# A hybrid decoder block on one core: the attention bias tables built on VectorE inside the first head pair, and small setup work issued earlier on ScalarE

## The chip, the core and the metric

The kernel runs on one NeuronCore of a Trainium2 chip: TensorE (PE), VectorE (DVE), ScalarE (ACT), GpSimd (POOL) and SyncE (SP, which here only issues transfers), 16 DMA engines, SBUF and the eight banks of PSUM. Each engine works through its own instructions in order, and they meet through semaphores. The metric is the device time of one execution in microseconds (us), the median of several runs.

## What is computed

One decoder layer over 256 tokens of width 1024: dilated window attention in three groups and retention side by side, merged through gates and an output projection, then a mixture of 32 experts in 4 groups, and a last RMSNorm. Cut to what matters:

```python
ATTN_GROUPS = ((128, 1), (512, 4), (2048, 16))      # (window, dilation)
h = rms_norm(x, g_mix)
proj = h @ w_in
qa, ka, va, qr, kr, vr, gr_swish, gate_a, gate_r = jnp.split(proj, split_at, axis=-1)
for gi, (window, dilation) in enumerate(ATTN_GROUPS):
    ...
    s = einsum(q, k) * (Dh ** -0.5)
    valid = (rel >= 0) & (rel <= n_back) & ...
    bias = -slopes * (rel * dilation)               # ALiBi, one slope for each of 8 heads
    s = jnp.where(valid, s + bias, -jnp.inf)
    ...
yr = retention_chunkwise(qr, kr, vr)                # decay gamma_h = 1 - 2^(-5-h)
merged = sigmoid(gate_a) * (o_attn @ w_attn_branch) + sigmoid(gate_r) * (o_ret @ w_ret_branch)
x = x + merged @ w_out
h2 = rms_norm(x, g_ffn)
x = x + hier_moe(h2, ...)                           # top-1 group, top-2 experts in it
return rms_norm(x, g_final)
```

With 256 tokens the bias of a group depends only on the distance query minus key: a query may see a key at distance d when 0 <= d <= window and d is a multiple of the dilation. The kernel therefore keeps one table `bias_t` (128 partitions x 3 groups x 256 positions) of minus the distance, or a very large negative number where the key may not be seen, and multiplies it by the slope of the head.

## The kernel before

**Precision.** Projections are made with float32 split in two: ACT rounds a chunk of weights to its high part (`high`, L589 to L596) and DVE subtracts it to get the low part (`low`, L762 to L770). PE then makes three products (high x high, high x low, low x high; `mm3`, L1159). The normed input is split the same way: ACT writes `hT` part 0 (`normed_high(m)`, L604) and DVE part 1 (`normed_low(m)`, L803), for m = 0 to 3, two of the eight 128-row tiles each.

**Units of work.** A "quad" Q is one block of weight columns in four chunks s = 0 to 3, each two of the eight row tiles. SP loads chunk s of quad Q+1 into the raw buffer s as soon as DVE has made the low part of chunk s of quad Q (L385). ACT may overwrite chunk s of the split buffer once PE has used it (`chunk_used`, L594). PE needs for chunk s of a quad the low part of the weights (`lo_ready`, L1183), and for quad 0 also the low part of `hT` (`hT_dve`, L1228). So each chunk goes SP, ACT, DVE, PE.

**The start.** x is loaded; ACT squares and sums it, POOL takes the power -1/2, DVE spreads the result over a diagonal, PE turns it into a row, ACT copies the row to `roots`. PE transposes x. DVE makes the normed tiles (`norm_columns(m)`, L796) from the transposed x and the roots; its order is norm columns 0 and 1, `normed_low(0)`, `low(0, 1)`, `normed_low(1)`, norm columns 2, `low(0, 2)`, `normed_low(2)`, norm columns 3, `low(0, 3)`, `normed_low(3)`. ACT goes `normed_high(m)`, then `high(0, m+1)`. PE fills its idle time with 26 products that nobody reads (`unread`, L1165), the last 18 of them between the roots and the first chunk of quad 0.

**The bias table.** POOL writes the distance as an integer and as a float table (L542, L543). DVE makes the residues of groups 1 and 2 and adds them times the mask value (L782 to L786), all before its first step of the normalisation. POOL cuts the tables to the window with `affine_select` (L566 to L577) after the powers -1/2 of the normalisation. DVE waits for `bias_done` (L819) ahead of the attention loop.

**Attention.** Four head pairs i = 0 to 3, each a query quad 3i, a key quad 3i+1 and a value quad 3i+2. DVE copies the keys `kT` out of PSUM between the second and third `low` of the value quad (L825 to L827), and PE's scores wait for that copy (`ak_ev`, L1237). Then come bias and maximum (DVE), exponent (ACT), scaling (DVE), transposes and the product with the values (PE). On DVE and ACT pairs 0 to 2 are a loop on the engine and pair 3 is written out.

**After it.** Retention in two rounds (`decay` tables from four exponents on ACT, L649 to L652), gates, attention branch, retention branch, output projection, router (whose weights `wr` DVE multiplies by the gain `gain_k`, L926 to L929), and then eight or more passes over teams of four experts, each of which loads 24 MB of weights. SP also loads quarters of the first experts' weights in between (`quarter`, L409).

## Time and profile before

| | us |
|---|---|
| time, median of 3 runs | 776.35 (775.78 to 776.81) |
| the profiled execution | 775.78, of which its span 774.0 |
| PE busy | 581.4 (75%) |
| DVE busy | 241.1 (31%) |
| ACT busy | 183.4 (24%) |
| POOL busy | 10.8 (1%) |
| DMA mean over the span | 329 GB/s |

The span runs from the first to the last instruction of the core; 1.78 us of the profiled execution lie around it. Up to about 333 us PE works nearly without a gap and the DMA engines are busy some two thirds of the time; after that the passes over the experts follow with the DMA engines full at about 425 GB/s and PE waiting in each pass. A row of the timeline shows start, duration, engine, line, operation, written<-read tiles, shape and count, and in brackets how long the engine had been idle and who released it. Instructions of an engine overlap by about 0.1 us in it.

### The profile page before, as it was taken

What the parts mean: (1) busy time and instruction counts of PE and PEld (TensorE: products, weight loads), DVE (VectorE), ACT (ScalarE), POOL (GpSimd) and SP (SyncE); (2) the same over time, 40 slices, a digit from 0 to 9 for tenths busy, and PEclk for the clock granted to TensorE, in tenths of its full rate; (3) what the DMA queues carried; (4) which work ended last, traced back from release to release, by engine and by line L of the source; (5) the groups of instructions that cost most, each with busy time, mean ns of one, the idle gap of its engine ahead of it and who ended that gap; (6) DMA issues with size and microseconds to landing.
All of it is one profiled execution on the core that took longest, in us unless ns stands there. A gap on an engine that the chain in (4) does not pass through costs nothing.

```text
span 774.0 us, 10791 instructions
## 1 busy us (share of the span) xinstructions
PE 581.4 (75%) x4329; PEld 403.8 (52%) x4329; DVE 241.1 (31%) x407; ACT 183.4 (24%) x250; POOL 10.8 (1%) x31
## 2 busy tenths in 40 slices
PE   8999999999999999992960970970870870790795
PEld 8999999989899999840420320320320320320331
DVE  7668486746554457551010010010010010000001
ACT  5455453644425434420000000000000000000002
POOL 3000000000000000000000000000000000000000
PEclk9999999999999999997985895895895895795799
DMA  8966949555537667989999999999999999999995
GB/s 240 274 173 184 273 139 318 163 169 164 168 113 225 221 207 263 364 345 420 431 425 424 431 430 421 432 425 425 428 429 425 428 427 428 426 429 429 424 415 210
DMA packets 86538, 254.84 MB, mean 329 GB/s; under 512 B 8432, under 2 KB 57584, under 8 KB 74608
## 3 DMA queue, kind: packets, MB, share of 16 engines
q1 hardware_dynamic: 84000, 254.30, 85.4%
q10 hardware_dynamic: 2512, 0.18, 0.2%
q8 instruction: 18, 0.29, 0.2%
q14 instruction: 8, 0.07, 0.0%
HBM read 253.41 MB, written 1.05 MB: 329 GB/s over the span
## 4 chain that ended last, share of the span: by engine, by line
PE 64%; DMA 30%; DVE 2%; ACT 2%; issue 1%; SPq 1%; POOL 0%; POOLq 0%; DVEq 0%; ACTq 0%
PE ps L1157 63%; DMA ring<-in_w_down 29%; DVE low_part L766 1%; ACT work L632 1%; ACT high_part L596 1%; DMA ring<-in_w_out 0%; DMA store<-in_x 0%; SPq L508 0%; PE ps L1253 0%; DVE work L960 0%; DVE mid L954 0%; PE ps L1281 0%; PE ps L1363 0%; POOL rstd L539 0%; DVE hn L1135 0%
## 5 line engine op out<-in xcount | busy, mean ns | idle before, releaser
L1157 PE MATMUL ps<-store,work 128*32 128x512 f32 x128 | 71.7, 720 | 176.3 <-DMA ring<-in_w_down 175.6
L1157 PE MATMUL ps<-ring,work 128*32 128x512 f32 x896 | 184.5, 611 | 0.0
L1157 PEld LDWEIGHTS ps<-store,work 128*32 128x32 f32 x128 | 15.6, 130 | 224.7 <-DMA ring<-in_w_down 165.0
L1157 PE MATMUL ps<-hT,split 128*128 128x256 f32 x768 | 93.6, 284 | 0.0
L1157 PEld LDWEIGHTS ps<-hT,split 128*128 128x128 f32 x768 | 92.6, 192 | 0.8 <-issue 0.7
L769 DVE TENSOR_TENSOR split<-ring,split 128x768 fp32r<-128x768 f32 (+1 forms) x72 | 73.9, 1044 | 53.8 <-ACT split L596 53.7
L1073 DVE TENSOR_TENSOR work<-ps,gain_s 128x512 f32<-128x512 f32 x16 | 11.1, 692 | 247.9 <-PE ps L1157 247.9
L596 ACT ACTIVATE split<-ring 128x768 fp32r<-128x768 f32 (+1 forms) x72 | 65.0, 915 | 70.2 <-PE ps L1157 50.4
L1157 PE MATMUL ps<-split,hT 128*128 128x384 f32 (+1 forms) x384 | 80.4, 365 | 0.0
L1157 PEld LDWEIGHTS ps<-split,hT 128*128 128x128 f32 x384 | 68.8, 188 | 7.8
L1157 PE MATMUL ps<-hT_slot,work 128*32 128x512 f32 x128 | 71.7, 720 | 0.0
L1157 PE MATMUL ps<-oRT_slot,work 128*32 128x512 f32 x128 | 71.7, 720 | 0.0
L728 ACT ACTIVATE work<-ps 128x512 f32<-128x512 f32 x16 | 9.6, 597 | 240.7 <-PE ps L1157 240.7
L1157 PEld LDWEIGHTS ps<-ring,work 128*32 128x32 f32 x896 | 46.3, 113 | 38.8 <-issue 38.8
L1157 PE MATMUL ps<-mid,work 128*32 128x512 f32 (+1 forms) x152 | 61.9, 560 | 0.0
L766 DVE TENSOR_TENSOR low_part<-ring,high_part 128x1024 fp32r<-128x1024 f32 x36 | 44.1, 1225 | 46.8 <-ACT high_part L596 46.7
L1157 PE MATMUL ps<-spare,work 128*32 128x512 f32 x128 | 56.4, 594 | 0.0
L596 ACT ACTIVATE high_part<-ring 128x1024 fp32r<-128x1024 f32 x36 | 38.1, 1058 | 53.6 <-DMA ring<-in_w_in 21.9
L1157 PE MATMUL ps<-hT,high_part 128*128 128x256 f32 x256 | 46.3, 284 | 0.0
L1080 DVE TENSOR_TENSOR work<-work,ps 128x512 f32<-128x512 f32 x8 | 5.5, 689 | 130.1 <-PE ps L1157 130.1
L1157 PEld LDWEIGHTS ps<-hT,high_part 128*128 128x128 f32 x256 | 40.0, 192 | 0.1
L1157 PEld LDWEIGHTS ps<-mid,work 128*32 128x32 f32 (+1 forms) x152 | 18.1, 122 | 40.1 <-issue 38.7
(197 smaller groups left out, 691.2 us busy)
## 6 DMA issues: line engine op xcount, KB each, us to landing
ring<-in_w_up SPq DMA_DIRECT2D x23, 2048.0 KB, 38.2
ring<-in_w_gate SPq DMA_DIRECT2D x18, 2048.0 KB, 24.9
ring<-in_w_in SPq DMA_DIRECT2D x80, 256.0 KB, 3.2
ring<-in_w_in SPq DMA_DIRECT2D x96, 192.0 KB, 4.2
mid<-in_w_up SPq DMA_DIRECT2D x8, 2048.0 KB, 34.1
store<-in_w_down SPq DMA_DIRECT2D x7, 2048.0 KB, 17.6
hT_slot<-in_w_down SPq DMA_DIRECT2D x6, 2048.0 KB, 21.8
oRT_slot<-in_w_down SPq DMA_DIRECT2D x6, 2048.0 KB, 26.2
```

Source lines behind the costliest of these rows:

```text
L596: act.activation(high_of, raw(s, n), ACT.Copy).then_inc(hi_ready, 1)
L632: act.activation(probsT[u], s_cols(u), ACT.Copy).then_inc(apt_act, 1)
L728: act.activation(yS[:, h * HALF:(h + 1) * HALF], bank(2 + h), ACT.Copy).then_inc(yS_ev[h], 1)
L766: dve.tensor_tensor(low_part[:, s, 0:n], raw(s, n), high_part[:, s, 0:n].bitcast(F32), ALU.subtract).then_inc(lo_ready, 1)
L769: dve.tensor_tensor(split[:, s, 1, 0:n], raw(s, n), split[:, s, 0, 0:n].bitcast(F32), ALU.subtract).then_inc(lo_ready, 1)
L1073: dve.tensor_tensor(xg[:, steps, :], bank(h).rearrange("p (k s) -> p k s", k=4), gain_s[:, steps].unsqueeze(2).to_broadcast([P, 4, P]), AL ...
L1080: dve.tensor_tensor(hid, sg, bank(3), ALU.mult).then_inc(hid_ready, 1)
L1157: return pe.matmul(o, lhsT=l, rhs=r, start=start, stop=stop, skip_group_check=shared)
```

## The change

It takes the bias table off POOL and makes it on DVE alone, in the head pair that first needs it, and moves some small work.

- POOL loses the float distance table and the four `affine_select`. DVE loses the six steps at its start and the wait for `bias_done`. A new function `bias_of(g)` makes the table of one group in a chain of 8 (group 0) or 5 (groups 1 and 2) instructions on 128x256, each waiting for the one before: convert, mask the residue, compare, add. Its calls stand on DVE in pair 0: group 0 after the second `low` of the key quad, group 1 after the fourth, group 2 between the first and second `low` of the value quad. Pair 0 is written out for this, and the loop runs over pairs 1 and 2.
- On ACT the order in quad 0 is now `normed_high(0)`, `normed_high(1)`, `high(0, 1)`, `normed_high(2)`, `high(0, 2)`, `normed_high(3)`, `high(0, 3)`. DVE's order there stays.
- Four small loads (router weights, router bias and the ffn gain in two layouts) and the four exponents of the decay tables move on ACT from the retention stage to right behind `high(0, 3)`, ahead of `high(1, 0)`.
- DVE multiplies the router weights by the gain right after attention rather than in the gates, and waits for the decay tables there.

The diff, without the line that names the three semaphores that fall away:

```diff
             pool.iota(dist_i[:, :], pattern=[[1, T]], base=-P, channel_multiplier=-1).then_inc(const_ready, 1)
-            pool.iota(dist, pattern=[[1, T]], base=-P, channel_multiplier=-1,
-                      allow_small_or_imprecise_dtypes=True).then_inc(dist_done, 1)
...
             inv_root(0)
-
-            for g, (window, _dil) in enumerate(GROUPS):
...
-                ins = pool.affine_select(out=bias_t[:, g, :], in_=dist if g == 0 else bias_t[:, g, :], compare_op=ALU.is_ge,
-                                         fill=MASKED, base=P, pattern=[[-1, T]], channel_multiplier=1)
-                if window < T:
-                    link(ins)
-                    ins = pool.affine_select(out=bias_t[:, g, :], in_=bias_t[:, g, :], compare_op=ALU.is_ge, fill=MASKED,
-                                             base=window - P, pattern=[[1, T]], channel_multiplier=-1)
-                ins.then_inc(bias_done, 1)
...
             act.activation(roots, bank(4, T), ACT.Copy).then_inc(roots_ev, 1)
-            for m in range(CH):
-                normed_high(m)
-                if m < CH - 1:
-                    high(0, m + 1, W_A)
+            normed_high(0)
+            normed_high(1)
+            high(0, 1, W_A)
+            normed_high(2)
+            high(0, 2, W_A)
+            normed_high(3)
+            high(0, 3, W_A)
+
+            act.dma_start(wr[:, :, :], w_router.rearrange("(k p) n -> p k n", p=P)).then_inc(s_wr, 16)
+            act.dma_start(br[:, :], b_router.partition_broadcast(P)).then_inc(s_wr, 16)
+            act.dma_start(gain_k[:, :], g_ffn.rearrange("(k p) -> p k", p=P),
+                          allow_slow_non_contiguous=True).then_inc(s_gk, 16)
+            act.dma_start(gain_s[:, :], g_ffn.rearrange("(p k) -> p k", k=KT)).then_inc(s_gk, 16)
+            act.wait_ge(age_done, 1)
+            for h in range(RET_HEADS):
+                act.activation(decay[:, h, :], age[:, :], ACT.Exp,
+                               scale=float(np.log1p(-2.0 ** (-5.0 - h)))).then_inc(decay_done, 1)
...
             dve.memset(all_ones, 1.0).then_inc(ones_done, 1)
-            dve.wait_ge(const_ready, 3)
-            dve.wait_ge(dist_done, 1)
-            for g in range(1, NG):
-                link(dve.tensor_single_scalar(resid_i, dist_i, GROUPS[g][1] - 1, ALU.bitwise_and))
-                link(dve.tensor_copy(resid_f, resid_i))
-                dve.scalar_tensor_tensor(bias_t[:, g, :], resid_f, MASKED, dist, ALU.mult, ALU.add).then_inc(dil_done, 1)
-                dve.wait_ge(dil_done, g)
+            dve.wait_ge(const_ready, 1)
...
-            dve.wait_ge(bias_done, NG)
+
+            def bias_of(g):
+                window, dil = GROUPS[g]
+                if g == 0:
+                    dve.wait_ge(const_ready, 3)
+                    link(dve.tensor_copy(dist, dist_i))
+                link(dve.tensor_single_scalar(resid_i, dist_i, dil - 1, ALU.bitwise_and))
+                link(dve.tensor_copy(resid_f, resid_i))
+                link(dve.scalar_tensor_tensor(bias_t[:, g, :], resid_f, MASKED, dist, ALU.mult, ALU.add))
+                for cmp, lim in ((ALU.is_gt, 0.0), (ALU.is_lt, float(-window))):
+                    if lim <= -T:
+                        continue
+                    link(dve.tensor_single_scalar(resid_f, dist, lim, cmp))
+                    link(dve.scalar_tensor_tensor(bias_t[:, g, :], resid_f, MASKED, bias_t[:, g, :],
+                                                  ALU.mult, ALU.add))
 
             def attention(i, n_next):
                 for s in range(CH):
                     low(3 * i + 1, s, W_A)
+                    if isinstance(i, int) and i == 0 and s % 2 == 1:
+                        bias_of(s // 2)
                 for s in range(CH):
+                    if isinstance(i, int) and i == 0 and s == 1:
+                        bias_of(2)
...
-            with dve.Fori(0, PAIRS - 1) as i:
+            attention(0, W_A)
+            with dve.Fori(1, PAIRS - 1) as i:
                 attention(i, W_A)
             attention(PAIRS - 1, W_R)
+
+            dve.wait_ge(s_wr, 32)
+            dve.wait_ge(s_gk, 32)
+            dve.tensor_tensor(wr[:, :, :], wr[:, :, :], gain_k[:, :].unsqueeze(2).to_broadcast([P, KT, NR]),
+                              ALU.mult).then_inc(wr_ready, 1)
+            dve.wait_ge(decay_done, RET_HEADS)
```

The same loads, exponents, product and wait disappear at their old places in the retention and gate stages.

ACT in quad 0, from the copy of the roots to the first chunk of the key quad (`split` is written by `high`, `hT` by `normed_high`, `normed_done` is counted by DVE's norm columns). Before:

```order
L610 ACTIVATE work<-ps 128x256 [waits roots_psum]
L606 ACTIVATE hT<-hn 128x512 [waits normed_done]
L596 ACTIVATE split<-ring 128x768 [waits raw_loaded1]
L606 ACTIVATE hT<-hn 128x512 [waits normed_done]
L596 ACTIVATE split<-ring 128x768 [waits raw_loaded2]
L606 ACTIVATE hT<-hn 128x512 [waits normed_done]
L596 ACTIVATE split<-ring 128x768 [waits raw_loaded3]
L606 ACTIVATE hT<-hn 128x512 [waits normed_done]
L640 UNCONDITIONAL_BRANCH
```

And of the change, at the same place:

```order
L591 ACTIVATE hT<-hn 128x512 [waits normed_done] x2
L581 ACTIVATE split<-ring 128x768 [waits raw_loaded1]
L591 ACTIVATE hT<-hn 128x512 [waits normed_done]
L581 ACTIVATE split<-ring 128x768 [waits raw_loaded2]
L591 ACTIVATE hT<-hn 128x512 [waits normed_done]
L581 ACTIVATE split<-ring 128x768 [waits raw_loaded3]
L604 DMA wr<-in_w_router 128x8x36
L605 DMA br<-in_b_router 128x36
L606 DMA gain_k<-in_g_ffn 128x8x1
L608 DMA gain_s<-in_g_ffn 128x8
L611 ACTIVATE decay<-age 128x256 [waits age_done]
L611 ACTIVATE decay<-age 128x256 x3
```

Each `high` of quad 0 now stands behind the `normed_high` of its own number, and the four loads and four exponents stand ahead of the key quad.

DVE in the value quad, from its first `low` to the copy of the keys (`mid`) and the `low` behind it. Before (this is the body of the loop over pairs):

```order
L769 TENSOR_TENSOR split<-ring,split 128x768 [waits hi_ready]
L764 REGISTER_ALU
L769 TENSOR_TENSOR split<-ring,split 128x768 [waits hi_ready]
L827 COPY mid<-ps 128x768 [waits chunk_used]
L764 REGISTER_ALU
L769 TENSOR_TENSOR split<-ring,split 128x768 [waits hi_ready]
```

And of the change, at the same place of pair 0:

```order
L756 TENSOR_TENSOR split<-ring,split 128x768 [waits hi_ready,dve_chain]
L806 TENSOR_SCALAR work<-work 128x256
L807 CAST work<-work 128x256 [waits dve_chain]
L808 SCALAR_TENSOR_TENSOR bias_t<-work 128x256 [waits dve_chain]
L812 TENSOR_SCALAR work<-work 128x256 [waits dve_chain]
L813 SCALAR_TENSOR_TENSOR bias_t<-work,bias_t 128x256 [waits dve_chain]
L756 TENSOR_TENSOR split<-ring,split 128x768 [waits hi_ready,dve_chain]
L826 COPY mid<-ps 128x768 [waits chunk_used]
```

The table of group 2 now stands between the first two splits of the value quad, ahead of the copy of the keys; the five instructions of group 1 stand the same way just before its first split, and the eight of group 0 after the second split of the key quad.

## Rows read from the trace of the kernel before

**Rows 1.** The page, span in 40 slices: granted TensorE clock in tenths.

```profile
PEclk9999999999999999997985895895895895795799
```

**Rows 2.** Chain of waits in order of time: start us, us, what.

```profile
8.32 22.83 PE ps L1157 x188
31.15 9.74 PE ps L1157 x66
...
141.22 51.18 PE ps L1157 x344
...
394.67 32.07 DMA ring<-in_w_down
```

**Rows 3.** Timeline of DVE and POOL in the start: start us, us, engine, line.

```profile
4.05 0.29 DVE L784 CAST work<-work 128x256 f32<-128x256 int32 x1
4.38 0.42 DVE L785 SCALAR_TENSOR_TENSOR bias_t<-work 128x256 f32<-128x256 f32 x1
5.63 0.15 DVE L789 TENSOR_SCALAR ms<-ss 128x1 f32<-128x1 f32 x1 [0.83 <-ACT work L602]
6.52 0.29 DVE L791 TENSOR_SCALAR work<-ident,rstd 128x128 f32<-128x128 f32 x1 [0.74 <-POOL rstd L539]
...
7.78 0.40 POOL L571 TENSOR_SCALAR_AFFINE_SELECT bias_t<-work 128x256 f32<-128x256 f32 x1
7.86 0.41 DVE L791 TENSOR_SCALAR work<-ident,rstd 128x128 f32<-128x128 f32 x1 [0.67 <-POOL rstd L539]
```

**Rows 4.** Timeline of quad 0: DVE, ACT and PE.

```profile
9.26 1.66 DVE L800 SCALAR_TENSOR_TENSOR hn<-ps,mix_k,work 128x256 f32<-128x256 f32 x4
...
11.56 0.96 DVE L769 TENSOR_TENSOR split<-ring,split 128x768 fp32r<-128x768 f32 x1
...
12.58 17.52 PE L1157 MATMUL ps<-hT,split 128*128 128x256 f32 x144
...
16.08 0.95 DVE L769 TENSOR_TENSOR split<-ring,split 128x768 fp32r<-128x768 f32 x1
16.20 0.63 ACT L606 ACTIVATE hT<-hn 128x512 fp32r<-128x512 f32 x1 [0.89 <-DVE hn L800]
16.74 0.83 ACT L596 ACTIVATE split<-ring 128x768 fp32r<-128x768 f32 x1
16.95 0.69 DVE L805 TENSOR_TENSOR hT<-hn,hT 128x512 fp32r<-128x512 f32 x1
```

**Rows 5.** Timeline of ACT where exponents and small loads stand before.

```profile
144.16 1.34 ACT L651 ACTIVATE decay<-age 128x256 f32<-128x256 f32 x4
...
155.26 0.40 ACTq L664 DMA_DIRECT2D gain_k<-in_g_ffn  x1
...
193.31 0.39 ACTq L661 DMA_DIRECT2D wr<-in_w_router  x1
193.46 1.01 ACT L658 ACTIVATE work<-ps 128x1024 f32<-128x1024 f32 x1
...
193.73 0.60 ACTq L662 DMA_DIRECT2D br<-in_b_router  x1
```

**Rows 6.** Timeline of SP, ACT and DVE around the keys of pair 0.

```profile
18.59 5.92 SPq L387 DMA_DIRECT2D ring<-in_w_in  x8
...
24.74 0.84 ACT L596 ACTIVATE split<-ring 128x768 fp32r<-128x768 f32 x1 [1.64 <-DMA ring<-in_w_in]
...
30.14 0.96 DVE L827 COPY mid<-ps 128x768 f32<-128x768 f32 x1 [2.39 <-PE ps L1157]
...
31.01 1.82 DVE L769 TENSOR_TENSOR split<-ring,split 128x768 fp32r<-128x768 f32 x2
```

**Rows 7.** Busy time by window: PE, PEld, DVE, ACT, POOL; then clock, DMA.

```profile
370.00:371.00 1.00, 1.00 (x8) 0.22 (x4) 0.00 (x0) 0.00 (x0) 0.00 (x0) 0.55 1.08 459
...
767.00:768.00 1.00, 1.00 (x3) 0.17 (x1) 1.00 (x5) 0.87 (x4) 0.00 (x0) 1.00 0.00 0
...
770.00:771.00 1.00, 0.00 (x0) 0.00 (x0) 0.53 (x2) 0.13 (x1) 0.00 (x0) 0.62 0.62 233
```

More of the change, by code:

```diff
@@ L254, in hybrid_block @@
         s_mix = sem("s_mix")
-        dist_done, dil_done, bias_done = sem("dist_done"), sem("dil_done"), sem("bias_done")
         ones_done, spread_done, roots_psum, roots_ev, normed_done = (sem("ones_done"), sem("spread_done"), sem("roots_psum"),
@@ L564, in _ @@
             inv_root(0)
-            for g, (window, _dil) in enumerate(GROUPS):
-                if g == 0:
-                    pool.wait_ge(dist_done, 1)
-                else:
-                    pool.wait_ge(dil_done, g)
-                ins = pool.affine_select(out=bias_t[:, g, :], in_=dist if g == 0 else bias_t[:, g, :], compare_op=ALU.is_ge,
-                                         fill=MASKED, base=P, pattern=[[-1, T]], channel_multiplier=1)
-                if window < T:
-                    link(ins)
-                    ins = pool.affine_select(out=bias_t[:, g, :], in_=bias_t[:, g, :], compare_op=ALU.is_ge, fill=MASKED,
-                                             base=window - P, pattern=[[1, T]], channel_multiplier=-1)
-                ins.then_inc(bias_done, 1)
             for i in range(TWOS):
@@ L647, in turned_high @@
                                ACT.Copy).then_inc(roT_hi, 1)
-            act.wait_ge(age_done, 1)
-            for h in range(RET_HEADS):
-                act.activation(decay[:, h, :], age[:, :], ACT.Exp,
-                               scale=float(np.log1p(-2.0 ** (-5.0 - h)))).then_inc(decay_done, 1)
             for i in range(TWOS):
@@ L660, in _ @@
                     turned_high(i - 1)
-                    act.dma_start(wr[:, :, :], w_router.rearrange("(k p) n -> p k n", p=P)).then_inc(s_wr, 16)
-                    act.dma_start(br[:, :], b_router.partition_broadcast(P)).then_inc(s_wr, 16)
-                else:
-                    act.dma_start(gain_k[:, :], g_ffn.rearrange("(k p) -> p k", p=P),
-                                  allow_slow_non_contiguous=True).then_inc(s_gk, 16)
-                    act.dma_start(gain_s[:, :], g_ffn.rearrange("(p k) -> p k", k=KT)).then_inc(s_gk, 16)
                 for s in range(CH):
@@ L886, in _ @@
                     low(Q_RET + 2 + 3 * i, s, W_R)
-                if i == 0:
-                    dve.wait_ge(decay_done, RET_HEADS)
                 for j in range(2):
@@ L925, in _ @@
                     turned_low(TWOS - 1)
-                    dve.wait_ge(s_wr, 32)
-                    dve.wait_ge(s_gk, 32)
-                    dve.tensor_tensor(wr[:, :, :], wr[:, :, :], gain_k[:, :].unsqueeze(2).to_broadcast([P, KT, NR]),
-                                      ALU.mult).then_inc(wr_ready, 1)
             for s in range(CH):
```

## The prediction, made before the change was run

> **What bounds the kernel now.** I read three views in this order. First the chain of waits, to see what stands on the path to the end. In the first 330 us it is PE almost alone: 22.83 us of products from 8.32 to 31.15, then 9.74 from the first scores on, and the same way up to a stretch of 51.18 us from 141.22 [rows 2]. Behind that come the passes over the experts, where the chain is made of transfers, as the 32.07 us from 394.67 [rows 2]. Second the page's slices: the granted clock is full through the first eighteen slices, so PE is not held back there by its clock [rows 1]. Third the timeline of the first 45 us, where the change works. The expert loads are released by the progress of PE and DVE (SP waits for `b_ready`, `chunk_used` and `x2_ev` before it asks for them), and nothing in the kernel is tied to a fixed time. So whatever delays PE in the first pair delays the end by as much, and the question is only whether PE is delayed.
>
> **The start: what falls away.** The old DVE steps for the bias end with the one at 4.38, at 4.80; the next DVE step, at 5.63, had been waiting 0.83 us for ACT's sum of squares [rows 3]. Taking them away frees nothing that anyone waits for: 0. POOL's selects stand behind its two powers and end before DVE asks for them: 0. One small gain shows: the spread of the second row block took 0.41 us at 7.86, beside a select that ran from 7.78 to 8.18, and 0.29 us at 6.52 with POOL done [rows 3]. This step is on the path to the roots, so 0.12 us come back, and everything behind starts 0.12 earlier. The Trainium skill (SBUF — State Buffer, section "SBUF: two separate sides") says that POOL and some forms of DVE instruction take a shared pair of ports in turn, the loser waiting to the end of the other's instruction. By that, the step would have lost the 0.32 us that the select still had to run, and the gain would be 0.3 and the sum below 4.7; the trace shows the direction, with 0.12.
>
> **Quad 0: the new order on ACT.** DVE's order has not changed: `low(0, m)` still stands ahead of `normed_low(m)` and of the next norm columns. But ACT now makes `high(0, m)` only behind `normed_high(m)`, which waits for norm columns m. The two engines now wait for each other by turns. A `high` starts 0.54 us behind the `normed_high` (16.20 to 16.74) and takes 0.83 [rows 4]; with 0.04 for the hand-over, `low` comes 1.41 us after the start of `normed_high`. First turn: the norm columns 0 and 1 end at 9.26 + 1.66 = 10.92, `normed_high(1)` starts at 10.96, `low(0, 1)` at 12.37 instead of 11.56 [rows 4]: 0.81 late. Second and third turn: `low(0, 3)` stood 0.12 us ahead of `normed_high(3)` (16.08 against 16.20) and now comes 1.41 behind it: 1.53 more, and the same for m = 2. In all `low(0, 3)` and `normed_low(3)` are 0.81 + 2 x 1.53 = 3.87 us late. What that costs PE: it begins quad 0 at 12.58, when its unread products are done, and runs 8 chunks in 17.52 us, 2.19 each [rows 4]. Chunk 3 is due at 12.58 + 3 x 2.19 = 19.15, and `normed_low(3)` ended at 16.95 + 0.69 = 17.64, so there are 1.51 us of slack. Now it ends at 21.51 and PE starts chunk 3 at 21.55: **2.40 us lost** on PE, surely, since both engines only repeat what they did.
>
> **Between quad 0 and the key quad: small loads and exponents on ACT.** `normed_high(3)` is now at 16.20 + 0.81 + 1.53 = 18.54, `high(0, 3)` runs from 19.08 to 19.91. The four loads cost ACT's queue 0.40, 0.39, 0.60 and, for the second layout of the gain, a fourth of the 0.60 kind: 2.0 us together [rows 5]. The queue runs ahead of the engine: the load at 193.31 is issued before the copy at 193.46 that stands ahead of it in the program [rows 5]. So they start near 18.6 and end at 20.6, partly beside `high(0, 3)`. The four exponents take 1.34 together [rows 5]: to 22.0. `high(1, 0)` follows from 21.9 to 22.75, and `low(1, 0)` starts at 22.8. Bounds: if the loads cost ACT nothing, 0.7 us earlier; if they are issued only after `high(0, 3)`, 1.3 later. I take the middle, since the row shows the queue running ahead. Both groups leave places where they cost nothing: PE runs on for 51.18 us from 141.22 without them [rows 2].
>
> **Key and value quads: the table on DVE.** From `low(1, 0)` on DVE has no gap left before the copy of the keys. Six splits stand before that copy; two back to back take 1.82, so 0.91 each: 5.46 us [rows 6]. The table has 18 instructions. Conversions, masks and compares (11) go by the step from 4.05 to 4.38, 0.33 us; the fused multiply-adds (7) by 0.42 and the same gap of 0.04, 0.46 us [rows 3]. That is 3.63 + 3.22 = 6.85 us. The copy of the keys then starts at 22.8 + 5.46 + 6.85 = 35.1, against 30.14, where it had waited 2.39 us for PE [rows 6]. PE is not the later one: chunk 2 of the keys waits for `low(1, 2)`, which ends at 22.8 + 1.82 + 3.03 + 0.91 = 28.6, and two chunks later the keys are done at 33.0. The scores follow the copy as before (31.15 behind 30.14), so PE's scores come **4.97 us later** than before, the 2.40 among them. The compare and the float mask have no row of their own: between 0.23 and 0.43 a step, which is 0.4 us either way. Does a load come too late? The first value chunk was asked for at 18.59 and ready at 24.74, 6.1 us [rows 6]. It is now asked for at 23.8, ready at 29.9, and DVE wants its high part at 31.4: 0.6 us spare. If the four small transfers crowd the engines it may cost up to 0.9.
>
> **After pair 0.** Pairs 1 to 3, retention, gates, projection and the expert passes see the same gaps as before, shifted. The product of the router weights is one short step in a stretch where DVE waits for PE. The loop that lost one turn: 0.
>
> **Sum.** 4.97 - 0.12 = 4.85 us. On the profiled execution 775.78 + 4.85 = 780.6. That execution was 0.57 below the median, 776.35, so the forecast of the median is **781.2 us**.
>
> **The rivals.**
> - *The table is hidden.* DVE has 11.6 us between 18.59 and 30.14 and only five splits in it, so 6.8 us are free, just what the table costs. If the table fills these waits, only quad 0's loss stays: 776.35 + 2.40 - 0.12 = 778.6. Against it: DVE starts the stage 5.2 us later than it did, the free time lies in the wrong places, and PE's lateness is only 2.40. Chance 0.11.
> - *More waits than counted*: late small loads (1.3), crowded transfers (0.9), or the clock. PE now has gaps of about 1.6 us before chunk 3 and 1.8 before the scores. In the rows the clock was still full in the microsecond in which PE stopped, 767 to 768, and fell within 770 to 771, over 2 us later; after the long wait near 367 half clock held until 370 to 371, some 3 us, which would cost 1.5 [rows 7]. The Trainium skill (TensorE: Matmul & The Clock Gate, section "HAM oscillation — how this bites in real kernels") holds that waits of PE bring the lower clock back. My gaps are shorter than the one in the rows, with products between them. This case gives 782.5 to 785.5, beyond 784 only if two come together. Chance 0.12.
> - *No change*: the splits in quad 0 were late by less than PE's slack of 1.51, and the table is hidden. It would need turns of under 0.5 us where the rows give 1.53. 776.3. Chance 0.04.
> - *Faster.* The work moved away from ACT had been on the path in retention. Its place is ACT at 144 and at 155 to 194, its price 1.34 + 2.0 = 3.3 us, and at the start the waits would have to stay within 1.51. It decides if PE ever waits for ACT's exponents or loads there: 776.35 - 3.3 - 0.12 = 772.9. Against it stands the unbroken stretch of PE [rows 2]. Chance 0.04.
>
> **How the numbers follow.** The forecast has 0.69. It alone spans 779.4 to 783.7: down by 0.7 and 0.4 and half a microsecond between executions, up by 1.3, 0.4 and as much. It leaves out more than 2 in 10, so the range goes down to the hidden table and up over most of the second rival: 778.4 to 784.0. A measurement of this kernel tells 0.2%, 1.55 us, from no change. Forecast and first two rivals are slower by more than that: 0.92; same 0.04; faster 0.04.
>
> **What would show it.** Right: in the profile after, `low(0, 3)` starts about 3.8 us later than 16.08; PE waits at chunk 3 for `hT`; the four loads and exponents stand between `high(0, 3)` and `high(1, 0)`; DVE has no idle time from `low(1, 0)` to the copy of the keys, which starts near 35.0; scores near 36.0; later stages keep their lengths. Wrong: `low(1, 0)` not near 22.7 (the loads), table instructions off 0.33 and 0.46, the granted clock below full before 330 us, or PE's lateness growing or shrinking behind pair 0.

## The result and the profile after

| | before | after |
|---|---|---|
| time, median of 6 runs | 776.79 us (775.78 to 778.31) | 781.0 us (780.4 to 781.46) |
| after / before, 95% interval | | 1.006 (1.005 to 1.007) |
| the profiled execution, its span | 775.78, 774.0 | 781.54, 779.8 |

The change costs 4.2 us of the median, by the interval 3.9 to 5.4. The forecast was 781.2.

The page of the kernel after: the engines' busy time, and below it the slices of the granted clock.

```profile
span 779.8 us, 10774 instructions
...
PE 583.7 (75%) x4329; PEld 403.5 (52%) x4329; DVE 244.4 (31%) x419; ACT 183.4 (24%) x250; POOL 8.3 (1%) x26
...
PEclk9999999999999999998895795795795795795799
```

POOL has lost 2.5 us of work and DVE has gained 3.3, ACT has the same as before; nothing in these sums says that the kernel is 4 us slower. The early slices of the clock are full in both kernels [rows 1]. The next view is the chain of waits in order of time (start us, us, what), first of the kernel after:

```profile
36.01 9.74 PE ps L1157 x66
...
146.07 51.18 PE ps L1157 x344
...
236.28 71.63 PE ps L1157 x588
...
338.41 15.30 PE ps L1157 x132
...
400.42 31.78 DMA ring<-in_w_down
```

and of the kernel before, the two places that [rows 2] does not hold:

```profile
231.42 60.26 PE ps L1157 x504
...
333.15 15.30 PE ps L1157 x132
```

Subtract place by place. The first scores are at 36.01 against 31.15 [rows 2], 4.86 later. The second place is 4.85 later (146.07 against 141.22), the third 4.86. So the whole difference arises ahead of the first scores, and PE carries it unchanged through four pairs and retention, into the gates. Behind the output projection it is 5.26, at the start of an expert's down weights 5.75, and in the span 5.8. The last 0.9 us is taken up with the experiments.

Where it arises, the timeline shows. A row has start, duration, engine, line, operation, tiles, count, and in brackets the idle time before it and who ended it. PE of the kernel after, from the first product of quad 0 to the scores:

```profile
12.53 4.55 PE L1157 MATMUL ps<-hT,split 128*128 128x256 f32 x36
17.77 2.41 PE L1157 MATMUL ps<-hT,split 128*128 128x256 f32 x18 [0.69 <-DVE hT L786]
21.55 7.00 PE L1157 MATMUL ps<-hT,split 128*128 128x256 f32 x54 [1.38 <-DVE hT L786]
28.73 4.57 PE L1157 MATMUL ps<-hT,split 128*128 128x256 f32 x36 [0.18 <-DVE split L756]
...
36.01 2.23 PE L1157 MATMUL ps<-mid 64*128 64x256 f32 x24 [1.66 <-DVE mid L826]
```

Before, this was one row of 144 products in 17.52 us [rows 4] with no gap. Now PE waits at chunk 2 and chunk 3 of quad 0 for `hT`, which DVE's `normed_low` writes, and then for `mid`, the copy of the keys. In between it waits 0.18 us at chunk 2 of the key quad (28.73) for a split that stands behind the table of group 0. And that copy no longer waits for PE. DVE of the same kernel, from its splits in quad 0 to the copy:

```profile
12.30 0.96 DVE L756 TENSOR_TENSOR split<-ring,split 128x768 fp32r<-128x768 f32 x1 [0.82 <-ACT split L581]
...
19.86 0.96 DVE L756 TENSOR_TENSOR split<-ring,split 128x768 fp32r<-128x768 f32 x1 [1.43 <-ACT split L581]
...
22.96 1.83 DVE L756 TENSOR_TENSOR split<-ring,split 128x768 fp32r<-128x768 f32 x2 [1.55 <-ACT split L581]
24.71 0.28 DVE L805 CAST work<-work 128x256 f32<-128x256 int32 x1
...
26.93 0.29 DVE L812 TENSOR_SCALAR work<-work 128x256 f32<-128x256 f32 x1
27.26 0.42 DVE L813 SCALAR_TENSOR_TENSOR bias_t<-work,bias_t 128x256 f32<-128x256 f32 x1
27.72 1.83 DVE L756 TENSOR_TENSOR split<-ring,split 128x768 fp32r<-128x768 f32 x2
...
34.13 0.96 DVE L756 TENSOR_TENSOR split<-ring,split 128x768 fp32r<-128x768 f32 x1
35.01 0.95 DVE L826 COPY mid<-ps 128x768 f32<-128x768 f32 x1
```

From 22.96 on no row of DVE has a bracket: the engine is never idle until the copy at 35.01, 12.05 us later. Before, the copy had waited 2.39 us for PE [rows 6]. In these rows one engine has taken the other's place as the bound, and everything that makes `low(1, 0)` start later now arrives at the scores.

### The profile page after: what moved, and what is told of

The parts are those of the page before. It is cut to its first block, busy times and chain, and to the rows that moved or that the text cites. A ratio compares the mean times of both kernels' runs of the same rounds, so it can differ in the third digit from the quotient of the medians.

```text
span 779.8 us, 10774 instructions
## 1 busy us (share of the span) xinstructions
PE 583.7 (75%) x4329; PEld 403.5 (52%) x4329; DVE 244.4 (31%) x419; ACT 183.4 (24%) x250; POOL 8.3 (1%) x26
## 4 chain that ended last, share of the span: by engine, by line
PE 62%; DMA 30%; DVE 4%; ACT 2%; issue 1%; SPq 1%; ACTq 0%; POOL 0%; POOLq 0%; DVEq 0%
PE ps L1157 61%; DMA ring<-in_w_down 28%; DVE split L756 1%; ACT work L630 1%; DMA ring<-in_w_out 1%; DMA store<-in_x 1%; SPq L507 0%; DVE hn L781 0%; PE ps L1253 0%; ACT split L581 0%; DVE low_part L753 0%; ACT high_part L581 0%; PE ps L1363 0%; DVE bias_t L813 0%; PE ps L1281 0%
```

## The experiments

All compute the same result as the kernel before; `table0_twice` makes one part of the table a second time. The first product of quad 0 stands at different times in different executions (12.53 in `after`, 12.16 in `table0_twice`, which differ only behind it), so besides the ratio I read one distance inside the trace: from the first product of quad 0 to the first scores. It is 18.57 before and 23.48 after, a difference of 4.91. It comes from one profiled execution of each kernel; the ratio comes from 4 to 12 runs, and its interval is 1.3 to 2.4 us wide, too wide to tell most of these kernels from one another by time alone. So the sizes below are read from the distance, and the ratio is only asked not to speak against it.

| | quad 0 | low(1, 0) | copy of keys | scores | distance | ratio to before (95%) |
|---|---|---|---|---|---|---|
| before | 12.58 | 17.60 | 30.14 | 31.15 | 18.57 | 1 |
| after | 12.53 | 22.96 | 35.01 | 36.01 | 23.48 | 1.006 (1.005 to 1.007) |
| order_only | 12.27 | 21.08 | 32.38 | 33.40 | 21.13 | 1.0026 (1.0016 to 1.0035) |
| small_only | 12.56 | 20.50 | 30.44 | 31.45 | 18.89 | 1.001 (1.0001 to 1.002) |
| table_only | 13.18 | 18.34 | 30.73 | 31.74 | 18.56 | 0.999 (0.9982 to 0.9999) |
| small_and_table | 12.24 | 20.32 | 32.37 | 33.37 | 21.13 | 1.003 (1.0019 to 1.004) |
| order_and_table | 12.54 | 21.35 | 33.40 | 34.40 | 21.86 | 1.0045 (1.0031 to 1.0059) |
| order_and_small | 12.48 | 22.83 | 32.78 | 33.80 | 21.32 | 1.0046 (1.0032 to 1.006) |
| table0_twice | 12.16 | 22.53 | 37.60 | 38.60 | 26.44 | 1.0107 (1.0092 to 1.0123) |
| loads_no_exps | 12.34 | 22.55 | 34.60 | 35.61 | 23.27 | 1.0061 (1.0046 to 1.0077) |
| exps_no_loads | 12.39 | 21.68 | 33.72 | 34.73 | 22.34 | 1.0057 (1.0042 to 1.0072) |
| table_less_filler | 11.27 | 17.19 | 29.24 | 30.25 | 18.98 | 0.9998 (0.9988 to 1.0007) |
| before_less_filler | 11.81 | 17.73 | 29.37 | 30.38 | 18.57 | 0.9987 (0.9978 to 0.9996) |

**Each part alone.** First the order of ACT in quad 0, in the kernel before:

```diff
-            for m in range(CH):
-                normed_high(m)
-                if m < CH - 1:
-                    high(0, m + 1, W_A)
+            normed_high(0)
+            normed_high(1)
+            high(0, 1, W_A)
+            normed_high(2)
+            high(0, 2, W_A)
+            normed_high(3)
+            high(0, 3, W_A)
```

> The kernel before with only the new order of high and normed_high on ACT in quad 0. Theory (turns of ACT and DVE in quad 0): chunk 3 of quad 0 starts at 21.5 us on PE instead of 19.15, the first scores at 33.5 instead of 31.15, and the time is 2.4 us longer (+0.3%). Rival (the waits in quad 0 are taken in by waits that PE has anyway behind it): scores at 31.2, no change of time.

PE and DVE of `order_only`, timeline:

```profile
21.29 11.05 PE L1160 MATMUL ps<-hT,split 128*128 128x256 f32 x90 [1.38 <-DVE hT L808]
...
32.38 0.96 DVE L830 COPY mid<-ps 128x768 f32<-128x768 f32 x1 [0.77 <-PE ps L1160]
```

The two waits of PE are those of the kernel after (0.68 at chunk 2, 1.38 here), and the copy stands behind PE again (idle 0.77, ended by PE). The distance grows by 2.56 and the time by 0.26%, about 2.0 us. The turns of ACT and DVE are real and cost by themselves a little more than the forecast's 2.40.

Then the small loads, the exponents and the router product alone, at their new places in the kernel before (the old places are emptied, as in the change):

```diff
+            act.dma_start(wr[:, :, :], w_router.rearrange("(k p) n -> p k n", p=P)).then_inc(s_wr, 16)
+            act.dma_start(br[:, :], b_router.partition_broadcast(P)).then_inc(s_wr, 16)
...
+            for h in range(RET_HEADS):
+                act.activation(decay[:, h, :], age[:, :], ACT.Exp,
+                               scale=float(np.log1p(-2.0 ** (-5.0 - h)))).then_inc(decay_done, 1)
+
             def attention(i, n_next):
```

> The kernel before with only the four small loads, the four exponents and the product of the router weights at their new places. Theory (ACT has slack ahead of the key quad when quad 0 keeps its order): normed_high(3) at 16.2, loads to 18.55, exponents to 19.9, low(1, 0) from 20.7 to 21.66 where PE would want it at 21.34: scores at most 0.4 us later, time +0.0 to +0.4 us. Rival (each part costs its share by itself): the 1.5 us between normed_low(3) and low(1, 0) in the changed kernel show here too, +1.5 us.

Timeline of ACT and DVE in `small_only`:

```profile
18.38 1.34 ACT L623 ACTIVATE decay<-age 128x256 f32<-128x256 f32 x4 [1.57 <-issue]
...
30.44 0.96 DVE L826 COPY mid<-ps 128x768 f32<-128x768 f32 x1 [1.55 <-PE ps L1156]
```

`low(1, 0)` starts 2.9 us later than before, and the copy still has 1.55 us of idle time, ended by PE. Of 2.9 us on ACT and DVE, 0.32 arrive at the scores: the small work is hidden nearly in full when it is moved alone. The 0.32 are lost inside the quads: PE's 144 products take 17.84 us instead of 17.52.

Last, the table alone: POOL's and DVE's old steps gone, `bias_of` in pair 0, ACT as before.

```diff
+                    if isinstance(i, int) and i == 0 and s % 2 == 1:
+                        bias_of(s // 2)
...
+                    if isinstance(i, int) and i == 0 and s == 1:
+                        bias_of(2)
```

> The kernel before with only the bias table made on DVE in pair 0. Theory (the table fills free time of DVE as long as low(1, 0) starts at 17.6): low(1, 0) at 17.6, 12.05 us of splits and table behind it less what overlaps, copy of the keys at 30.1, scores at 31.1 to 31.3, time within 0.3 us of before. Rival (the table costs its own share, the parts add up to 4.86): scores 1 to 2.5 us later, time +1 to +2.5 us.

Timeline of PE and DVE in `table_only`:

```profile
13.18 17.52 PE L1155 MATMUL ps<-hT,split 128*128 128x256 f32 x144
...
30.73 0.96 DVE L824 COPY mid<-ps 128x768 f32<-128x768 f32 x1
```

PE makes its 144 products in 17.52 us with no gap, ends at 30.70, and the copy follows at once. The distance is 18.56 against 18.57. All of the table's 6.8 us on DVE lie beside PE's work. So the rival "the table is hidden" describes this kernel rightly, and was wrong only for the table behind a DVE that starts late. The ratio, 0.999, is below one by more than the distance explains. Of its 0.8 us the faster spread of the second row block (below, in the part on the prediction) is worth 0.12; for the rest I have no cause.

The three alone add 2.56, 0.32 and -0.01 to the distance, 2.87 together, and the change adds 4.91. **The parts do not add up**, so the pairs are needed.

**One part left out.** `small_and_table` is the change with the old order of ACT:

```diff
-            normed_high(0)
-            normed_high(1)
-            high(0, 1, W_A)
...
+            for m in range(CH):
+                normed_high(m)
+                if m < CH - 1:
+                    high(0, m + 1, W_A)
```

> The changed kernel with the old order of high and normed_high on ACT in quad 0, so small loads, exponents and table moved. Theory (a chain on DVE that starts with low(1, 0)): low(1, 0) at 20.7, and 12.05 us behind it, as between 22.96 and 35.01 in the changed kernel, the copy of the keys at 32.75, scores at 33.75: +2.6 us against before, 2.3 us less than the changed kernel. Rival (the parts add up): the sum of small_only and table_only; by the theory's own numbers for those two that would be only +0.0 to +0.7 us.

The copy of the keys in `small_and_table` (timeline), with no idle time of DVE before it:

```profile
32.37 0.95 DVE L823 COPY mid<-ps 128x768 f32<-128x768 f32 x1
```

Two parts that alone add 0.31 add 2.56 together. The copy comes 12.05 us behind `low(1, 0)` (20.32 to 32.37), as in the kernel after (22.96 to 35.01).

`order_and_table` leaves out the small loads, exponents and router product:

```diff
-            act.dma_start(wr[:, :, :], w_router.rearrange("(k p) n -> p k n", p=P)).then_inc(s_wr, 16)
-            act.dma_start(br[:, :], b_router.partition_broadcast(P)).then_inc(s_wr, 16)
...
-            for h in range(RET_HEADS):
-                act.activation(decay[:, h, :], age[:, :], ACT.Exp,
-                               scale=float(np.log1p(-2.0 ** (-5.0 - h)))).then_inc(decay_done, 1)
```

> The changed kernel with small loads, exponents and router product back at their old places. Theory: ACT is done with high(1, 0) before normed_low(3) ends at 21.4, so low(1, 0) starts at 21.35 instead of 22.96; 12.05 us behind it the copy of the keys at 33.4, scores at 34.4: 1.6 us less than the changed kernel, +3.3 us against before. Rival (what ACT does ahead of the key quad is hidden by quad 0's waits): the same as the changed kernel, scores at 36.0.

`low(1, 0)` at 21.35, the copy at 33.40: 12.05 again. PE's key quad ended at 32.62, so DVE is the later by 0.8. Distance 21.86.

`order_and_small` has the table made on POOL and at DVE's start, as before:

```diff
-                    if isinstance(i, int) and i == 0 and s % 2 == 1:
-                        bias_of(s // 2)
...
-                    if isinstance(i, int) and i == 0 and s == 1:
-                        bias_of(2)
```

> The changed kernel with the bias table back on POOL and at the start of DVE. Theory: PE loses 2.4 us in quad 0; low(1, 0) starts at 22.96 and ends at 23.9, just as PE asks for it; the key quad then runs unbroken to 32.7 and the copy of the keys follows at 32.7, scores at 33.7: +2.5 us against before. Rival (the small loads and exponents cost PE time by themselves also without the table): scores at 35 or later.

DVE of `order_and_small`, timeline:

```profile
32.78 0.96 DVE L829 COPY mid<-ps 128x768 f32<-128x768 f32 x1 [1.28 <-PE ps L1159]
```

Without the table `low(1, 0)` is as late as in the change (22.83), and the copy waits for PE all the same. Distance 21.32, hardly more than the order alone. (The ratio, 1.0046, is higher than that of the order alone, 1.0026, but the two intervals overlap; in the profiled execution the surplus lies behind the first scores, where the same stages differ between all these kernels, see "What stays over".) Putting the table back costs 2.16 here (23.48 less 21.32) and nothing in the kernel before.

All rows fit one rule: **the copy of the keys starts at the later of two times, the end of PE's key quad and `low(1, 0)` + 12.05 us when the table stands in between.** Before the change `low(1, 0)` is at 17.60, and 17.60 + 12.05 = 29.65 is half a microsecond ahead of 30.14. The table alone just fits; each microsecond by which ACT delays `low(1, 0)` beyond that half one arrives in full.

**Testing the rule.** If DVE bounds the copy, more table work must arrive in full. `table0_twice` is the change with the group 0 table made a second time:

```diff
                     if isinstance(i, int) and i == 0 and s % 2 == 1:
                         bias_of(s // 2)
+                        if s == 1:
+                            bias_of(0)
```

> The changed kernel with the eight instructions of the table of group 0 made twice, the second time right behind the first. Theory (DVE is the bound from low(1, 0) to the copy of the keys): the chain grows by 24.71 to 27.72 = 3.0 us, the copy of the keys at 38.0, scores at 39.0, time +3.0 us against the changed kernel. Rival (DVE still has free time there and PE or a load is later): less than 1.5 us.

Timeline of PE in `table0_twice`:

```profile
31.32 5.86 PE L1159 MATMUL ps<-hT,split 128*128 128x256 f32 x36 [3.19 <-DVE split L756]
...
38.60 2.23 PE L1159 MATMUL ps<-mid 64*128 64x256 f32 x24 [0.37 <-DVE mid L828]
```

Eight instructions took 3.02 us of DVE (27.29 to 30.31), the copy comes 15.07 us behind `low(1, 0)` instead of 12.05, and the distance grows by 2.96. The full price arrives. The ratio to before goes from 1.006 to 1.0107, some 3.6 us, with about a microsecond of interval on each.

The rule also says that the table alone should cost something once PE has less to do. `table_less_filler` is `table_only` with four of PE's unread products taken out ahead of quad 0:

```diff
             pe.wait_ge(normed_done, 2)
-            unread(10)
+            unread(6)
```

> table_only with 6 instead of 10 unread products before quad 0. Theory (PE begins quad 0 when the filler ends, at 12.58, while normed_low(0) ended at 11.53): the 8 entries less of some 0.115 us let quad 0 start at 11.65, chunk 3 would be due at 18.2 with normed_low(3) ready at 17.6; the key quad ends at 29.2, but the table keeps the copy of the keys at 30.1, so scores at 31.1: no gain from it here, within 0.3 us of before. Rival (PE's start alone sets the scores): 0.9 us faster, scores at 30.2.

Timeline of PE and DVE in `table_less_filler`:

```profile
11.27 17.52 PE L1155 MATMUL ps<-hT,split 128*128 128x256 f32 x144
17.19 1.83 DVE L754 TENSOR_TENSOR split<-ring,split 128x768 fp32r<-128x768 f32 x2
...
29.24 0.95 DVE L824 COPY mid<-ps 128x768 f32<-128x768 f32 x1
...
30.25 2.23 PE L1155 MATMUL ps<-mid 64*128 64x256 f32 x24 [0.41 <-DVE mid L824]
```

The clock time of the expectation was missed, since this execution began earlier and `low(1, 0)` stood at 17.19, not 17.6. The rule held to the hundredth: 17.19 + 12.05 = 29.24. PE had ended its key quad at 28.79 and then waited 0.41 us for the copy. So the slack of half a microsecond is used up, and the table is what bounds. The scores' clock time, 30.25, happens to be the rival's 30.2; it is the wait of 0.41 us and the distance, 18.98 against 18.57, that speak against the rival, by which PE's start alone would set the scores.

The same edit in the kernel before, without the table, is `before_less_filler`:

```diff
             pe.wait_ge(normed_done, 2)
-            unread(10)
+            unread(6)
```

> The kernel before with 6 instead of 10 unread products ahead of quad 0. Theory (PE's start is set by the filler, and nothing behind it in pair 0 is late by as much): quad 0 starts at 11.65 instead of 12.58, chunk 3 is due at 18.2 with normed_low(3) ready at 17.64, the copy of the keys follows PE at 29.2, scores at 30.2, 18.57 us behind quad 0's start as before; time 0.9 us less (-0.12%, at the edge of what the rounds can tell). Rival (a transfer or DVE sets the scores): the distance grows to 19 us or more and the time stays.

DVE of `before_less_filler`:

```profile
29.37 0.96 DVE L827 COPY mid<-ps 128x768 f32<-128x768 f32 x1 [1.60 <-PE ps L1157]
```

The copy waits for PE (1.60 us), the distance stays at 18.57, and quad 0 begins 0.77 us earlier than in the kernel before, with the granted clock at 1.00 over the first 50 us. The time is 776.17 against 777.02 on that chip, ratio 0.9987 (0.9978 to 0.9996). It is the fastest by ratio of the kernels here, about 0.8 to 1.0 us faster than the kernel before and by the ratios some 5.7 us faster than the kernel after. Against the kernel before, that is inside the 0.2% that the prediction took as the limit of telling, though the interval lies below one.

**Which of the small things costs.** `loads_no_exps` puts the four exponents (and DVE's product and waits) back, `exps_no_loads` the four loads (and the same):

```diff
-            act.wait_ge(age_done, 1)
-            for h in range(RET_HEADS):
-                act.activation(decay[:, h, :], age[:, :], ACT.Exp,
-                               scale=float(np.log1p(-2.0 ** (-5.0 - h)))).then_inc(decay_done, 1)
```

> The changed kernel with the four exponents (and the router product) back at their old places; the four small loads stay ahead of the key quad. Theory (ACT cannot start high(1, 0) before its queue has issued the loads, 2.34 us from normed_high(3) on): high(1, 0) at 20.85, low(1, 0) at 21.7 instead of 22.96, 12.05 us from there to the copy of the keys, so 1.2 us off the changed kernel; first product of quad 0 to first score 22.3 us instead of 23.48. Rival (the issue of the loads runs beside the engine and costs nothing, the exponents are all of it): low(1, 0) right behind normed_low(3) at 21.35, 21.86 us as without both.

ACT and its queue in `loads_no_exps`, timeline (the rows named ACTq are issues of transfers, their duration is that of the issue):

```profile
19.34 1.04 ACTq L606 DMA_DIRECT2D gain_k<-in_g_ffn  x1
20.41 0.96 ACTq L608 DMA_DIRECT2D gain_s<-in_g_ffn  x1
...
21.67 2.32 ACT L581 ACTIVATE split<-ring 128x768 fp32r<-128x768 f32 x3 [2.03 <-issue]
```

By the theory 1.2 us should have come back, and 0.21 did (distance 23.27). The two issues of the gain took 1.04 and 0.96 us here, against 0.46 and 0.80 in the kernel after, so that the four loads held the queue from 18.28 to 21.37, and ACT stood idle for 2.03 us (19.64 to 21.67), nearly all of it while they were issued. The last issue ended 9.03 us behind the first product of quad 0, against 8.28 in the kernel after (20.81 less 12.53). Without these 0.75 us the distance would be about 22.5, by my estimate from these rows, near the 22.3 of the theory. Why the issues were longer stays open. The rival, that issues run beside the engine and cost nothing (21.86), falls.

```diff
-            act.dma_start(wr[:, :, :], w_router.rearrange("(k p) n -> p k n", p=P)).then_inc(s_wr, 16)
-            act.dma_start(br[:, :], b_router.partition_broadcast(P)).then_inc(s_wr, 16)
-            act.dma_start(gain_k[:, :], g_ffn.rearrange("(k p) -> p k", p=P),
-                          allow_slow_non_contiguous=True).then_inc(s_gk, 16)
-            act.dma_start(gain_s[:, :], g_ffn.rearrange("(p k) -> p k", k=KT)).then_inc(s_gk, 16)
```

> The changed kernel with the four small loads (and the router product) back at their old places; the exponents stay ahead of the key quad. Theory: exponents 19.75 to 21.05 behind high(0, 3), high(1, 0) from 21.0 to 21.85, low(1, 0) at 21.85: 1.1 us off the changed kernel, first product of quad 0 to first score 22.4 us. Rival (the loads are all of it): 21.86 us as without both. Together with the run beside it: by the theory the two do not add up (1.2 and 1.1 alone, 1.6 together), since either one alone already frees ACT nearly in time for normed_low(3).

Timeline of `exps_no_loads`:

```profile
19.59 1.32 ACT L606 ACTIVATE decay<-age 128x256 f32<-128x256 f32 x4
21.68 1.83 DVE L757 TENSOR_TENSOR split<-ring,split 128x768 fp32r<-128x768 f32 x2 [0.40 <-ACT split L581]
```

The exponents now start right behind `high(0, 3)`, the distance falls to 22.34, 1.14 below the change. So, taken back one at a time, the loads are worth 1.14 us and the exponents 0.21; but the 0.21 is one execution with long issues, and by the estimate above it would be about 1 with issues of the length in the kernel after. By the medians these two cannot be told from the change (781.2 and 781.39 against 777.02 on their chip).

**What stays over.** In the profiled execution of the change the output projection's last row of products starts at 319.93, against 314.67 before: 5.26 later, where 236.28 was 4.86 later. The added 0.4 arises at one place: the conversion of a chunk of the projection's weights on ACT, for which the kernel after had to wait. The transfer in the chain of the kernel after, then that row of ACT after and before (timeline):

```profile
308.31 5.03 DMA ring<-in_w_out
```

```profile
313.36 1.06 ACT L581 ACTIVATE high_part<-ring 128x1024 fp32r<-128x1024 f32 x1 [0.37 <-DMA ring<-in_w_out]
```

```profile
308.12 1.04 ACT L596 ACTIVATE high_part<-ring 128x1024 fp32r<-128x1024 f32 x1
```

The transfer was asked for 4.81 us later than before (307.92 against 303.11), as everything was; before, it had landed when ACT came to it, and here ACT waited 0.37 us. Why it took longer is open. It does not follow the edits: in the kernels with single parts the chain has such a transfer at 304 to 307 us as well, 4.94 us (`order_only`), 5.07 (`small_only`) and 6.21 (`table_only`), and the longest stands in the kernel whose time did not grow. Seven of the thirteen kernels have a row in their chain some 200 us behind the first scores (231.42 before, 236.28 after), and up to there they agree within 0.1 us. From the first scores to the row of 132 products ahead of the experts (333.15 before, 338.41 after) all thirteen take 301.90 to 304.84 us, with 302.00 before and 302.40 after, and from there to the end of the span 440.8 to 441.4, with 440.85 before and 441.39 after. So the 0.4 us and the 0.5 us behind it are no larger than what the kernels differ by in stages that, but for the place of the router product, none of the edits touches. That they are variation between executions fits this, but no second profile of the same kernel shows it. The medians, 4.2 us apart (3.9 to 5.4), leave room for the 4.9 of the first scores and at most half a microsecond more.

## Why the prediction was right, point by point

- **What bounds the kernel.** PE's chain carries a delay of the start to the end: 4.86, 4.85 and 4.86 at three places up to 236 us. Right.
- **The spread, 0.12 us back.** The second spread of the kernel after has 0.29 us instead of 0.41, on a row that the trace gives as follows (timeline of DVE):

```profile
7.92 0.29 DVE L772 TENSOR_SCALAR work<-ident,rstd 128x128 f32<-128x128 f32 x1 [0.67 <-POOL rstd L538]
```

  The duration was right. The step started 0.06 later than before, so it ended 0.06 earlier, and the first product of quad 0 came 0.05 earlier, which is less than executions with the same start differ by (12.16 to 12.53). The cause is shown by the other kernels: the step takes 0.41 us in all five that keep POOL's select beside it, and 0.28 or 0.29 in all eight that have none. The rule of the Trainium skill that was weighed (SBUF — State Buffer, section "SBUF: two separate sides"), by which 0.32 us would have been lost to the select, is not borne out by these rows: 0.12 were.
- **Quad 0.** Forecast: DVE's last split of quad 0 near 19.95 less 0.12, and 2.40 us lost at chunk 3. Measured: 19.86, and chunk 3 at 21.55 where 12.53 + 3 x 2.19 = 19.10 was due, 2.45 lost. The forecast did not name that a part of it, 0.69, falls at chunk 2 already. `order_only` has the same two waits by itself.
- **Small loads and exponents.** Forecast 2.0 us of issue and `low(1, 0)` near 22.7. The rows of ACT in the kernel after (ACTq is its queue):

```profile
18.47 0.40 ACTq L604 DMA_DIRECT2D wr<-in_w_router  x1
18.90 0.60 ACTq L605 DMA_DIRECT2D br<-in_b_router  x1
...
19.53 0.46 ACTq L606 DMA_DIRECT2D gain_k<-in_g_ffn  x1
20.01 0.80 ACTq L608 DMA_DIRECT2D gain_s<-in_g_ffn  x1
20.86 1.34 ACT L611 ACTIVATE decay<-age 128x256 f32<-128x256 f32 x4 [1.04 <-issue]
```

  The queue does run ahead of the engine, as taken: the loads begin with `normed_high(3)` at 18.46. They take 2.34 us, 0.34 more than the sum, above all the second layout of the gain (0.80 for 0.60). `low(1, 0)` is at 22.96, 0.3 late.
- **The table.** Forecast 5.46 + 6.85 = 12.31 us from `low(1, 0)` to the copy. Measured 12.05: the six splits take 5.26 (two in 1.75, one in 0.88) and the 18 instructions 6.79, by steps of 0.33 and 0.46 as taken (26.93 to 27.26 to 27.72). The compare, which had no row before, has 0.29 us, as the other short ones.
- **Sum.** The 0.3 late and the 0.26 short cancel. Copy at 35.01 (forecast 35.1 less 0.12), scores at 36.01. The sum of 4.85 was right to 0.01 at the scores, with two terms off by 0.3 in opposite directions; that much luck is in it. There is more in the median, 781.0 for a forecast of 781.2: the medians lie 4.2 us apart and not 4.85, and the median of the kernel before is 776.79 and not the 776.35 from which the forecast started. Two sums of the range are slips. By its own terms the forecast alone spans 779.6 to 783.4 (written 779.4 to 783.7), and the second rival reaches 784.9 (written 785.5), since 1.3, 0.9 and 1.5 add up to 3.7. Neither touches the result.
- **The clock.** The granted clock is full from 12 to 50 us in spite of PE's gaps. The kernel after by window (engine busy times as in [rows 7], then the clock):

```profile
12.00:50.00 38.00, 33.77 (x277) 32.07 (x276) 32.16 (x59) 19.24 (x32) 0.00 (x0) 1.00 0.64 183
```

- **The rivals.** "The table is hidden" holds for `table_only`, where the distance does not change, and falls for the change. "More waits than counted": the loads had 0.34 of its 1.3. The transfers cost nothing: the first value chunk was ready at 29.68 (forecast 29.9), DVE came to it at 31.36 without a wait, and the 0.9 us of that rival had no row behind it. The clock cost nothing either. "No change" and "faster" fall with 4.86 us at the first scores; that ACT's work had been off the path in retention shows in the equal lengths from 146.07 to 236.28 (90.21 in the kernel after, 90.20 before).

## What to carry to other kernels

Where two engines meet, compute for each the time at which it arrives, and cost an edit by the later one: a step with 0.5 us of slack is free once. Here one edit cost 2.56 us alone and two hid nearly in full (0.32 and nothing), and the three together cost 2.04 us more than the sum. Moving work "into idle time" needs that idle time to lie behind the moment at which the engine is first late; when an order upstream delays the engine's start, the idle time it had is gone before the moved work arrives. Test for it by pairs, not by parts alone: `small_and_table` told in one run what three single parts could not.

## What the runs showed of the hardware that was not expected

**The clock behind a wait.** The prediction feared half clock behind PE's gaps. Gaps of 1.38 and 1.66 us in the kernel after left it full. In `table0_twice` PE had a gap of 3.19 us, and the windows of that kernel (columns as in [rows 7]) show what came behind it:

```profile
30.00:31.00 1.00, 0.00 (x0) 0.00 (x0) 0.96 (x2) 0.00 (x0) 0.00 (x0) 0.92 0.00 0
31.00:32.00 1.00, 0.68 (x3) 0.68 (x4) 1.00 (x2) 0.00 (x0) 0.00 (x0) 0.50 0.00 0
32.00:33.00 1.00, 1.00 (x7) 1.00 (x7) 0.93 (x4) 0.00 (x0) 0.00 (x0) 0.50 0.35 95
33.00:34.00 1.00, 1.00 (x6) 1.00 (x6) 0.90 (x4) 0.00 (x0) 0.00 (x0) 0.50 1.11 318
34.00:35.00 1.00, 1.00 (x10) 1.00 (x9) 1.00 (x2) 0.00 (x0) 0.00 (x0) 0.87 0.87 209
35.00:36.00 1.00, 1.00 (x11) 1.00 (x10) 0.90 (x4) 0.85 (x1) 0.00 (x0) 1.00 1.04 256
```

PE had stopped at 28.13. The clock fell to 0.50, the 1.2 GHz level, near the end of the wait (the row from 30 to 31 has 0.92 in the mean), and half clock held over the first 3 us of work or so: from 31.32 into the microsecond from 34 to 35, whose mean is 0.87. The 36 products took 5.86 us instead of 4.57, a loss of 1.29 on PE. It did not reach the end, since PE ended its key quad at 37.18 and DVE came to the copy only at 37.60. The Trainium skill (TensorE: Matmul & The Clock Gate, section "HAM oscillation — how this bites in real kernels") says that waits of PE bring the lower clock back. The trace agrees for the gap of 3.19 us. Behind the gaps of 1.38 and 1.66 us, shorter than the waits that section describes, the clock stayed full.

**The issue of a small load.** The same load on ACT's queue took different times to issue in different kernels, one execution of each: the gain in its first layout 0.46 us (after, `small_only`) and 1.04 (`loads_no_exps`), in its second layout 0.80 (after), 0.60 (`small_only`) and 0.96 (`loads_no_exps`). ACT was idle for 1.04, 1.57 and 2.03 us (after, `small_only`, `loads_no_exps`) before it could go on, mostly while the last loads were being issued. What sets the length, and whether it goes with the kernel or only with the execution, is open.
